# Running the first four weight tiles of a stage together, input chunk by input chunk, in a one-core transformer kernel

## The chip, the cores and the metric

The kernel runs on one core of a Trainium2 chip. The metric is the time of one execution on the device in microseconds (us). The core's engines are called PE (TensorE, matmuls), DVE (VectorE), ACT (ScalarE), POOL (GpSimd) and SP (SyncE, which issues most DMAs); ACTq and SPq are the queues that issue DMAs.

## The reference, cut to what matters

`x` is 512 tokens by 1024 features. Two blocks run one after the other, then a hybrid mixer, a cross attention over a memory of 256 tokens, and a gated feed-forward. Every matrix product that the change touches takes the output of an RMS norm:

```python
y = x * rsqrt(mean(x * x, axis=-1) + eps) * g       # the norm
h = modulate(y, shift, scale)                       # in the first two blocks
# block 0: nsa_mixer(h): h @ w_in (1024 x 2608), rotary, three attentions, @ w_out
# block 1: swa_sink_mixer(h): q, k, v = h @ w_in (1024 x 1280), rotary, window attention, @ w_out
a = relu(h @ w_up); y = (a * a) @ w_down            # MLP of both blocks, 4096 hidden
proj = h @ w_in_2; q = h @ wq; kv = mem_n @ wkv     # hybrid mixer, cross attention
h @ ffn_w_up_2                                      # feed-forward, 2 x 2816
```

## The kernel before, in words

Activations are held transposed, as eight **chunks** of 128 features by 512 tokens. fp32 accuracy comes from splitting: a chunk is a rounded high part `ah` and a rest `al`, a weight a high part `wh` and a rest `wl`. A **unit** is a weight tile of 1024 x 128; its product takes, for each of the eight chunks, three matmuls (lines 702 to 704: wh by ah, wl by ah, wh by al), so 24 in one PSUM bank. There are some 309 units, and they pass through a ring of four slots (`RING = 4`): SP loads `raw` (L533), ACT rounds it to `wh` (L1806, in `highs`, which first waits until the unit four before has been used), POOL subtracts to get `wl` (L642), PE multiplies (`gemm`, L720, unit by unit, chunks inside), DVE evacuates the bank. PE waits in `bank_free` for the bank of four units before, and on `lo_done` for the weights.

`norm` on DVE (L1176) makes the chunks one at a time: L1184 scales, ACT rounds (L1843 or L1845), L1198 or L1196 makes the rest and signals `a_ready`. `gemm` with `ready=` waits for each chunk in turn, so the first unit after a norm goes at the pace of the norm.

What hangs on a unit's end differs by stage. In the two MLPs (`mlp`, L925 on PE, L1457 on DVE, L1976 on ACT) eight "up" units are followed at once by eight "down" units that read the hidden chunks. For each "up" unit DVE does relu (L1465), square (L1467), waits for ACT's rounding to `hh` (L1985), and subtracts to `hl` (L1469), which signals `hid_made`; in the first MLP it also adds one modulation step (L1488, L1491). ACT's order is written out: round the weights of unit c+4, then wait for DVE's square of unit c, then `hh` of c. In the sliding-window stage (`swa_in`) pairs of units are rotated by DVE (`rotary`, L1304 to L1318), ACT rounds them and issues their writes to DRAM (`rotated`, L1867 to L1879: 8 DMAs of 256 KB for k, 4 for each of the four q pairs), and SP waits for the k and first q writes before it loads them back (L536, L540) and before it issues the next weight tiles. In `nsa_in` ACT writes the first rotated pair and units 3 and 4 to scratch (L1896, L1900), and SP waits for both before it issues the loads that follow.

At a stage's end `highs_and_squares` (L1821) does for each of the last eight units: `highs` of unit c+4, then the square of the evacuated chunk c. `root` (L1829) takes the square root of their sum.

Of the kernel before, what the change touches and what calls it, by code (L numbers as in the profile page):

```python
# [73 lines left out]
def place_of_units():  # L74

    n = {name: FIRST[name] for name, _ in STAGES}
    of = list(range(UNITS))

    def stage(name, runs):
        got = [n[name] + a + k for a, count in runs for k in range(count)]  # L80
        of[n[name]:n[name] + len(got)] = got
    stage("nsa_in", ((0, 4), (12, 4), (16, 4), (20, 1), (4, 8)))
    stage("swa_in", ((8, 2), (10, 1), (0, 8)))
    for name in ("mlp0", "mlp1"):
        stage(name, [(8 * b, 8) for b in (0, 2, 1, 4, 3, 6, 5, 7)])
    stage("ffn", ((0, 16), (32, 8), (16, 16), (52, 8), (40, 12), (60, 8)))
    assert sorted(of) == list(range(UNITS))
    return of
# [151 lines left out]
def build(nc, src, out):  # L240
# [30 lines left out]
    cond = at("cond", k1 + 0.375, [P, DC])  # L271
    coef = at("coef", k1 + 0.4375, [P, 2, 6, DC])
    eps = at("eps", k1 + 0.875, [P, 1])
    neg_sinks = at("neg_sinks", k1 + 0.9375, [P, HEADS])
    ident_r = at("ident_r", k1 + 1, [P, P], F32R)
    mask_r = at("mask_r", k1 + 1.5, [P, 2, P], F32R)
# [412 lines left out]
    def _(pe):  # L689
# [30 lines left out]
        def gemm(first, count, high, low, turned=False, tokens=S, ks=DC, ready=None):  # L720
# [13 lines left out]
            over_units(pe, first, first + count, one)  # L734
            done[0] += count

        def gemm_pairs(first, pairs, high, low, tokens=S):

            for u in range(first, first + 2 * pairs, 2):
                n, slot = done[0], u % RING
                pe.wait_ge(lo_done, u + 2)
                for i in range(tokens // P):
                    if i % 2 == 0:
                        bank_free(n + i // 2)
                    o = ps[:, (n + i // 2) % RING, i % 2 * 256:i % 2 * 256 + 256].rearrange("p (a f) -> p a f", a=2)
                    t = slice(i * P, (i + 1) * P)
                    for k in range(DC):
                        nc.tensor.matmul(o, high[:, k, t], wh[:, slot:slot + 2, k], start=k == 0, stop=False)  # L750
                        nc.tensor.matmul(o, high[:, k, t], wl[:, slot:slot + 2, k], start=False, stop=False)
                        mm = nc.tensor.matmul(o, low[:, k, t], wh[:, slot:slot + 2, k], start=False, stop=k == DC - 1)
                mm.then_inc(unit_used, 2)
                done[0] += tokens // P // 2
# [170 lines left out]
        def mlp(name, hid0):  # L925
            u = FIRST[name]
            for b, (what, grp) in enumerate(MLP_BLOCKS):

                def sums():
                    if name == "mlp0" and b:  # L930
                        pe.wait_ge(adc_used, 8 * b)
                        ada(ps[:, 6, 8 * b:8 * b + 8], acc_mlp[:, (b - 1) % 2])
                if what == "up":
                    gemm(u, 4, ah, al, ready=(a_ready, A_READY[name]))
                    sums()
                    gemm(u + 4, 4, ah, al)
                elif b == 7:
                    gemm_squared(u, hh, hl, 0, ready=(hid_made, hid0 + 8 * grp), midway=sums)
                else:
                    gemm(u, 4, hh, hl, ready=(hid_made, hid0 + 8 * grp))  # L940
                    sums()
                    gemm(u + 4, 4, hh, hl)
                u += 8
# [10 lines left out]
            ada(ps[:, 7, 8 * k:8 * k + 8], acc_in)  # L954

        u = FIRST["nsa_in"]
        gemm(u, RING, ah, al, ready=(a_ready, 0))
        gemm(u + RING, 4, ah, al)
        gemm_pairs(u + 8, 2, ah, al)
        ada_in_sum(0)  # L960
# [28 lines left out]
        square_sums()  # L989
        mlp("mlp0", 0)  # L990
        square_sums()
        gemm(FIRST["swa_in"], 2, ah, al, ready=(a_ready, A_READY["swa_in"]))
        gemm(FIRST["swa_in"] + 2, 1, ah, al, turned=True)
        gemm(FIRST["swa_in"] + 3, 8, ah, al)
        attention(PLAN_SWA)
        gemm_squared(FIRST["swa_out"], ah, al, 0, ready=(o_split, 2 * GROUPS))
        square_sums()
# [1 line left out]
        square_sums()  # L999

        u = FIRST["mix_in"]
        gemm(u, 7, ah, al, ready=(a_ready, A_READY["mix_in"]))

        pe.wait_ge(evac, done[0] - 6)
        for c in range(2):
# [64 lines left out]
        head_spread(3)  # L1070
        gemm_squared(FIRST["mix_out"], ah, al, 1, ready=(mix_ready, 0))

        gemm(FIRST["xq"], 8, ah, al, ready=(a_ready, A_READY["xq"]))
        square_sums(MEM)
        gemm(FIRST["kv"], 7, mh, ml, tokens=MEM, ready=(a_ready, A_READY["mem"]))
        gemm_pairs(FIRST["kv"] + 7, 4, mh, ml, tokens=MEM)
        gemm(FIRST["kv"] + 15, 1, mh, ml, tokens=MEM)
        pe.wait_ge(evac, done[0])
# [36 lines left out]
        for what, grp in FFN_BLOCKS:  # L1115
            n = FF_GROUPS[grp]
            if what == "up":
                gemm(u, 2 * n, ah, al, ready=(a_ready, A_READY["ffn"]))
                u += 2 * n
            else:  # L1120
                ready = (hid_made, 64 + sum(FF_GROUPS[:grp]))
# [8 lines left out]
    def _(dve):  # L1130
# [430 lines left out]
        ada_read_out(11, ps[:, 6, 56:64])  # L1561
        ada_coef(1, 5)
        rotary(pair_s)
        v.tensor_copy(vv[:, 0, :, 0:P], bank().rearrange("p (i f) -> p i f", i=SC)).then_inc(evac, 1)
        for _ in range(4):
            rotary(pair_s, query=True)
        attention(PLAN_SWA)
        copy_out()
# [218 lines left out]
    def _(act):  # L1787
# [33 lines left out]
        def highs_and_squares(u, out_t, bank0):  # L1821

            for c in range(DC):
                highs(u + RING + c, u + RING + c + 1)
                squares(out_t[:, c:c + 1], (evac, lambda _: bank0 + c + 1), count=1,
                        added=6 * summed[0] + max(c - 2, 1) if c >= 2 else None)
            summed[0] += 1
# [180 lines left out]
        u = FIRST["swa_in"]  # L2008
        highs(u + RING, u + RING + 2)
        rotated(6, pair_s)  # L2010
        highs(u + RING + 2, u + RING + 3)
        for p in range(4):
            highs(u + RING + 3 + 2 * p, u + RING + 5 + 2 * p)
            rotated(7 + p, pair_s, grp=p)
        n += UNITS_SWA_IN
        attention(PLAN_SWA)
# [221 lines left out]
```

## Time and profile before

| | us |
|---|---|
| median of three runs | 2417.26 (2416.27 to 2418.76) |
| the profiled execution, its own time | 2418.09 |
| its span in the trace | 2416.3 |
| PE busy | 2104.6 (87%) |
| DVE busy | 1137.4 (47%) |
| POOL busy | 901.5 (37%) |
| ACT busy | 693.4 (29%) |

The granted TensorE clock was 0.904 of full speed on the mean. A matmul's busy time overlaps the next one's, so a busy PE is not one at its peak, and the shares are a mean over stages with different limits.

### The profile page before, as it was taken

The page shows a single profiled execution, that of the slowest core. Times are in us where ns is not written, and L with a number is a line of the kernel's source. Part 1 is how long each engine was busy: PE and PEld are TensorE (multiplying, and loading weights), DVE is VectorE, ACT ScalarE, POOL GpSimd, SP SyncE. Part 2 cuts the span into 40 slices and gives each one's busy share as a digit, 9 for nine tenths or more (in the row PEclk, how much of TensorE's full clock was granted, in tenths as well). Part 3 has the DMA queues.
Part 4 walks back from the last instruction along what each step waited for, and adds up shares of the span by engine and source line. Part 5 has one row for each costly group of instructions (what it writes and reads, how often), then busy time and mean ns, then how long its engine had stood idle before and what let it go on. Part 6 is the DMA issues. An engine that isn't in the chain of part 4 may idle for free.

```text
span 2416.3 us, 27295 instructions
## 1 busy us (share of the span) xinstructions
PE 2104.6 (87%) x10492; PEld 1722.9 (71%) x10492; DVE 1137.4 (47%) x1672; ACT 693.4 (29%) x1195; POOL 901.5 (37%) x513
## 2 busy tenths in 40 slices
PE   2968679997999997958799999797689878999997
PEld 2766667775888885846588888676577646888886
DVE  6424545637564564444544244336432224626354
ACT  2112244533222223135322222323132313222222
POOL 1223244432544542256244444333034403444442
PEclk9968569997999997979899999899699879999998
DMA  6543521222655540432133333222022302333331
GB/s 245 193 156 104 189 86 47 71 71 87 200 184 177 195 141 27 149 134 83 53 96 96 96 96 96 78 70 79 1 96 89 113 9 79 96 96 96 96 96 61
DMA packets 79770, 255.33 MB, mean 106 GB/s; under 512 B 10536, under 2 KB 11048, under 8 KB 79272
## 3 DMA queue, kind: packets, MB, share of 16 engines
q1 hardware_dynamic: 70480, 237.86, 29.8%
q10 hardware_dynamic: 9176, 15.89, 1.9%
q8 instruction: 79, 1.29, 0.2%
q14 instruction: 35, 0.29, 0.0%
HBM read 235.21 MB, written 18.51 MB: 105 GB/s over the span
## 4 chain that ended last, share of the span: by engine, by line
PE 46%; issue 29%; POOL 11%; DVE 7%; DMA 3%; ACT 2%; ACTq 1%; SPq 0%; POOLq 0%; DVEq 0%
PE ps L702 11%; PE ps L704 11%; PE ps L703 11%; POOL wl L642 10%; PE ps L911 2%; DMA raw<-in_units 2%; PE ps L857 2%; PE ps L883 2%; DMA qscr<-rot_ls 1%; POOL pr L663 1%; PE ps L1108 1%; PE ps L842 1%; DVE tt L1184 1%; PE ps L1085 1%; ACTq L1875 1%
## 5 line engine op out<-in xcount | busy, mean ns | idle before, releaser
L642 POOL TENSOR_TENSOR wl<-raw,wh 128x1024 fp32r<-128x1024 f32 x309 | 764.2, 2477 | 1371.5 <-ACT wh L1806 1371.5
L1806 ACT CAST wh<-raw 128x1024 fp32r<-128x1024 f32 x309 | 323.4, 1051 | 1286.4 <-PE ps L704 1031.6
L702 PE MATMUL ps<-ah,wh 128*128 128x512 f32 x1496 | 596.5, 399 | 30.0 <-DVE al L1198 18.7
L703 PE MATMUL ps<-ah,wl 128*128 128x512 f32 x1496 | 588.4, 393 | 0.0
L704 PE MATMUL ps<-al,wh 128*128 128x512 f32 x1496 | 588.2, 393 | 0.0
L702 PEld LDWEIGHTS ps<-ah,wh 128*128 128x128 f32 x1496 | 284.2, 190 | 107.4 <-issue 21.1
L704 PEld LDWEIGHTS ps<-al,wh 128*128 128x128 f32 x1496 | 284.6, 190 | 60.3
L703 PEld LDWEIGHTS ps<-ah,wl 128*128 128x128 f32 x1496 | 285.2, 191 | 56.9 <-issue 0.7
L702 PE MATMUL ps<-hh,wh 128*128 128x512 f32 x688 | 269.2, 391 | 4.0 <-DVE hl L1763 4.0
L703 PE MATMUL ps<-hh,wl 128*128 128x512 f32 x688 | 268.2, 390 | 0.0
L704 PE MATMUL ps<-hl,wh 128*128 128x512 f32 x688 | 268.2, 390 | 0.0
L1469 DVE TENSOR_TENSOR hl<-rs,hh 128x512 fp32r<-128x512 f32 x64 | 135.6, 2119 | 43.9 <-ACT hh L1985 43.9
L702 PEld LDWEIGHTS ps<-hh,wh 128*128 128x128 f32 x688 | 129.5, 188 | 32.0 <-DVE hl L1763 5.2
L704 PEld LDWEIGHTS ps<-hl,wh 128*128 128x128 f32 x688 | 129.5, 188 | 27.2
L703 PEld LDWEIGHTS ps<-hh,wl 128*128 128x128 f32 x688 | 129.6, 188 | 26.7
L857 PE MATMUL ps<-ks,qs 128*128 128x256 f32 (+3 forms) x384 | 95.8, 356 | 28.0 <-ACT pr L1941 14.7
L1941 ACT ACTIVATE pr<-ps,st 128x512 f32<-128x512 f32 (+1 forms) x192 | 94.3, 504 | 68.5 <-DVE st L1375 47.2
L1375 DVE TENSOR_REDUCE st<-ps 128x1 f32<-128x512 f32 (+1 forms) x192 | 78.2, 449 | 51.3 <-PE ps L860 43.9
L661 POOL TENSOR_SCALAR pr<-pr,st,gates 128x512 f32<-128x512 f32 (+3 forms) x128 | 75.9, 608 | 57.5 <-DVE st L1402 56.9
L857 PEld LDWEIGHTS ps<-ks,qs 128*128 128x128 f32 x384 | 65.3, 210 | 38.4 <-issue 17.4
L1476 DVE TENSOR_TENSOR y<-ps,y 128x512 f32<-128x512 f32 x32 | 22.1, 692 | 123.1 <-PE ps L704 123.1
L762 PE MATMUL ps<-sq,sm 128*32 128x128 f32 x440 | 33.8, 393 | 52.7 <-ACT sq L1818 48.0
(270 smaller groups left out, 2617.4 us busy)
## 6 DMA issues: line engine op xcount, KB each, us to landing
raw<-in_units SPq DMA_DIRECT2D x309, 512.0 KB, 3.5
ada_mlp<-in_ada SPq DMA_DIRECT2D x56, 512.0 KB, 3.4
ada_in<-in_ada SPq DMA_DIRECT2D x24, 512.0 KB, 7.7
ada<-in_ada SPq DMA_DIRECT2D x16, 512.0 KB, 5.3
qs<-qscr SPq DMA_DIRECT2D x32, 256.0 KB, 2.7
ks<-kscr SPq DMA_DIRECT2D x12, 512.0 KB, 3.9
x<-in_xT SPq DMA_DIRECT2D x1, 2048.0 KB, 13.3
kscr<-rot_h ACTq DMA_DIRECT2D x8, 256.0 KB
```

The costliest lines, as they stand in the source:

```text
L642: nc.gpsimd.tensor_tensor(wl[:, slot], raw[:, slot], wh[:, slot].bitcast(F32), ALU.subtract).then_inc(lo_done, 1)
L661: op = nc.gpsimd.tensor_scalar(o, o, st[:, 2, n % 4, i:i + 1], gates[:, i, c:c + 1], ALU.mult, ALU.mult)
L702: nc.tensor.matmul(out_ap, wh[:, slot, k], high[:, k0 + k], start=first and k == 0, stop=False)
L703: nc.tensor.matmul(out_ap, wl[:, slot, k], high[:, k0 + k], start=False, stop=False)
L704: mm = nc.tensor.matmul(out_ap, wh[:, slot, k], low[:, k0 + k], start=False, stop=last and k == ks - 1)
L857: nc.tensor.matmul(o, qs[:, j, i * P:(i + 1) * P], ks[:, slot, part, k0 * P:k1 * P], start=part == 0, stop=False)
L883: mm = nc.tensor.transpose(ps[:, plan.t_bank + b, col + c * P:col + (c + 1) * P], pr[:, n % 3, at0:at0 + P], small("ident"))
L911: mm = nc.tensor.matmul(ps[HD * h:HD * h + HD, bank, q[0] * P:(q[-1] + 1) * P], vv[:, kind, kb, col_v:col_v + HD], pt[:, n[h] % 4, place[k ...
L1375: op = v.tensor_reduce(st[:, 0, s, i:i + 1], ps[:, plan.s_bank(w, b), col:col + (k1 - k0) * P], X, ALU.max, negate=True)
L1469: v.tensor_tensor(hl[:, c], t, hh[:, c].bitcast(F32), ALU.subtract).then_inc(hid_made, 1)
L1806: a.copy(wh[:, slot], raw[:, slot]).then_inc(hi_done, 1)
L1941: a.activation(pr[:, n % 3, b * S + col:b * S + col + width], ps[:, plan.s_bank(w, b), col:col + width], ACT.Exp, bias=shift[:, i:i + 1], ...
```

## The change

A new function `gemm_wide` multiplies several units with the chunks as the outer loop. It is used for the first four units after each of the eight norms (for the kv product with 256 tokens). In `swa_in` the order of units becomes k, k, q, q, v, q x6 instead of k, k, v, q x8, with PE's, DVE's and ACT's order changed to fit. One ACT instruction, a square root of `eps` into a new [128, 1] tile `warm`, is put between `highs` and `squares` of the last unit in `highs_and_squares`.

```diff
-    stage("swa_in", ((8, 2), (10, 1), (0, 8)))
+    stage("swa_in", ((8, 2), (0, 2), (10, 1), (2, 6)))
...
+        def gemm_wide(first, count, high, low, ready, tokens=S):
+
+            n0 = done[0]
+            pe.wait_ge(lo_done, first + count)
+            for i in range(count):
+                bank_free(n0 + i)
+            for k in range(DC):
+                pe.wait_ge(ready[0], ready[1] + k + 1)
+                for i in range(count):
+                    o, slot = ps[:, (n0 + i) % RING, 0:tokens], (first + i) % RING
+                    nc.tensor.matmul(o, wh[:, slot, k], high[:, k], start=k == 0, stop=False)
+                    nc.tensor.matmul(o, wl[:, slot, k], high[:, k], start=False, stop=False)
+                    mm = nc.tensor.matmul(o, wh[:, slot, k], low[:, k], start=False, stop=k == DC - 1)
+                    if k == DC - 1:
+                        mm.then_inc(unit_used, 1)
+            done[0] += count
...
-                    gemm(u, 4, ah, al, ready=(a_ready, A_READY[name]))
+                    if b == 0:
+                        gemm_wide(u, 4, ah, al, (a_ready, A_READY[name]))
+                    else:
+                        gemm(u, 4, ah, al)
...
-        gemm(FIRST["swa_in"], 2, ah, al, ready=(a_ready, A_READY["swa_in"]))
-        gemm(FIRST["swa_in"] + 2, 1, ah, al, turned=True)
-        gemm(FIRST["swa_in"] + 3, 8, ah, al)
+        gemm_wide(FIRST["swa_in"], 4, ah, al, (a_ready, A_READY["swa_in"]))
+        gemm(FIRST["swa_in"] + 4, 1, ah, al, turned=True)
+        gemm(FIRST["swa_in"] + 5, 6, ah, al)
...
         rotary(pair_s)
+        rotary(pair_s, query=True)
         v.tensor_copy(vv[:, 0, :, 0:P], bank().rearrange("p (i f) -> p i f", i=SC)).then_inc(evac, 1)
-        for _ in range(4):
+        for _ in range(3):
...
                 highs(u + RING + c, u + RING + c + 1)
+                if c == DC - 1:
+                    a.activation(warm[:], eps[:], ACT.Sqrt)
                 squares(out_t[:, c:c + 1], (evac, lambda _: bank0 + c + 1), count=1,
...
         highs(u + RING, u + RING + 2)
         rotated(6, pair_s)
-        highs(u + RING + 2, u + RING + 3)
         for p in range(4):
-            highs(u + RING + 3 + 2 * p, u + RING + 5 + 2 * p)
+            highs(u + (6, 8, 11, 13)[p], u + (8, 11, 13, 15)[p])
             rotated(7 + p, pair_s, grp=p)
```

The same replacement of the first `gemm` by `gemm_wide` stands at `nsa_in`, `mix_in`, `xq`, `kv` and `ffn`.

## Rows read from the trace of the kernel before

**Rows 1.** The page's busy time by engine, and its group of matmuls on L704.

```profile
PE 2104.6 (87%) x10492; PEld 1722.9 (71%) x10492; DVE 1137.4 (47%) x1672; ACT 693.4 (29%) x1195; POOL 901.5 (37%) x513
...
L704 PE MATMUL ps<-al,wh 128*128 128x512 f32 x1496 | 588.2, 393 | 0.0
```

**Rows 2.** Windows: us, busy time (count) by engine, granted PE clock, DMA share, GB/s.

```profile
572.43:598.10 25.67, 25.32 (x97) 19.19 (x97) 21.66 (x24) 8.63 (x11) 7.47 (x3) 0.88 0.24 82
583.59:597.19 13.60, 13.60 (x61) 11.26 (x60) 11.10 (x10) 3.79 (x5) 7.03 (x3) 1.00 0.45 154
1196.73:1222.39 25.66, 24.26 (x97) 18.41 (x98) 18.78 (x21) 8.63 (x11) 7.46 (x3) 0.94 0.17 44
1852.61:1867.33 14.72, 14.72 (x97) 14.10 (x98) 5.91 (x15) 5.17 (x8) 6.31 (x3) 0.80 0.17 48
```

**Rows 3.** Timeline of PE at the start of the first MLP (start, duration).

```profile
573.00 0.63 PE L703 MATMUL ps<-ah,wl 128*128 128x512 f32 x1
573.42 0.63 PE L704 MATMUL ps<-al,wh 128*128 128x512 f32 x1
```

**Rows 4.** Timeline of DVE, ACT, POOL after the first MLP's first unit (start, duration).

```profile
581.97 0.69 DVE L1465 TENSOR_SCALAR rs<-ps 128x512 f32<-128x512 f32 x1 [1.12 <-PE ps L704]
582.02 1.05 ACT L1806 CAST wh<-raw 128x1024 fp32r<-128x1024 f32 x1 [2.41 <-PE ps L704]
582.69 0.69 DVE L1467 TENSOR_TENSOR rs<-rs 128x512 f32<-128x512 f32 x1
583.15 2.49 POOL L642 TENSOR_TENSOR wl<-raw,wh 128x1024 fp32r<-128x1024 f32 x1 [31.67 <-ACT wh L1806]
583.42 0.62 ACT L1985 CAST hh<-rs 128x512 fp32r<-128x512 f32 x1 [0.34 <-DVE rs L1467]
584.07 2.12 DVE L1469 TENSOR_TENSOR hl<-rs,hh 128x512 fp32r<-128x512 f32 x1 [0.69 <-ACT hh L1985]
```

**Rows 5.** Timeline of DVE within the first MLP, and of POOL and DVE in nsa_in.

```profile
861.92 1.27 DVE L1491 SCALAR_TENSOR_TENSOR acc_mlp<-ada_mlp,cond,acc_mlp 128x1024 f32<-128x1024 f32 x1
863.21 0.69 DVE L1465 TENSOR_SCALAR rs<-ps 128x512 f32<-128x512 f32 x1
...
233.96 4.63 POOL L642 TENSOR_TENSOR wl<-raw,wh 128x1024 fp32r<-128x1024 f32 x1 [13.44 <-ACT wh L1806]
...
233.70 2.71 DVE L1347 SCALAR_TENSOR_TENSOR xb_l<-x,sm,xb_h 128x124 fp32r<-128x124 f32 x8
```

**Rows 6.** Timeline of DVE and ACT in nsa_in, after its second unit.

```profile
72.40 0.69 DVE L1304 TENSOR_TENSOR pair<-ps,trig 128x512 f32<-128x512 f32 x1 [6.66 <-PE ps L704]
...
77.08 1.66 ACTq L1896 DMA_DIRECT2D cscr<-pair  x2
...
83.26 1.28 ACTq L1900 DMA_DIRECT2D cscr<-vtmp  x2
```

**Rows 7.** Timeline in swa_in: k rotation, k writes, q reads, first score matmul.

```profile
976.47 0.69 DVE L1304 TENSOR_TENSOR pair_s<-ps,trig 128x512 f32<-128x512 f32 x1 [4.70 <-PE ps L704]
...
986.51 8.39 ACTq L1879 DMA_DIRECT2D kscr<-rot_ls  x4
...
1022.58 1.81 SPq L536 DMA_DIRECT2D qs<-qscr  x4
...
1043.85 0.58 PE L857 MATMUL ps<-ks,qs 128*128 128x256 f32 x1 [13.28 <-DVE pair_s L1307]
```

**Rows 8.** ACT at the end of nsa_out and of the second MLP, and all loads of L1833.

```profile
548.01 1.04 ACT L1806 CAST wh<-raw 128x1024 fp32r<-128x1024 f32 x1 [3.86 <-PE ps L704]
548.96 0.62 ACT L1818 ACTIVATE sq<-y 128x512 f32<-128x512 f32 x1
549.61 1.28 ACT L1833 ACT_TABLE_LOAD   x1
550.90 0.37 ACT L1833 ACTIVATE rs<-ps,eps 128x128 f32<-128x128 f32 x1
...
1551.16 0.37 ACT L1833 ACTIVATE rs<-ps,eps 128x128 f32<-128x128 f32 x1 [0.55 <-PE ps L762]
...
L1833 ACT ACT_TABLE_LOAD  x5: 1283/1283/1283, 24.2 to 2403.1; - x5
```

More of the change, by code:

```diff
@@ L273, in build @@
     eps = at("eps", k1 + 0.875, [P, 1])
+    warm = at("warm", k1 + 0.90625, [P, 1])
     neg_sinks = at("neg_sinks", k1 + 0.9375, [P, HEADS])
@@ L956, in _ @@
         u = FIRST["nsa_in"]
-        gemm(u, RING, ah, al, ready=(a_ready, 0))
+        gemm_wide(u, RING, ah, al, (a_ready, 0))
         gemm(u + RING, 4, ah, al)
@@ L1001, in _ @@
         u = FIRST["mix_in"]
-        gemm(u, 7, ah, al, ready=(a_ready, A_READY["mix_in"]))
+        gemm_wide(u, 4, ah, al, (a_ready, A_READY["mix_in"]))
+        gemm(u + 4, 3, ah, al)
         pe.wait_ge(evac, done[0] - 6)
@@ L1071, in _ @@
         gemm_squared(FIRST["mix_out"], ah, al, 1, ready=(mix_ready, 0))
-        gemm(FIRST["xq"], 8, ah, al, ready=(a_ready, A_READY["xq"]))
+        gemm_wide(FIRST["xq"], 4, ah, al, (a_ready, A_READY["xq"]))
+        gemm(FIRST["xq"] + 4, 4, ah, al)
         square_sums(MEM)
-        gemm(FIRST["kv"], 7, mh, ml, tokens=MEM, ready=(a_ready, A_READY["mem"]))
+        gemm_wide(FIRST["kv"], 4, mh, ml, (a_ready, A_READY["mem"]), tokens=MEM)
+        gemm(FIRST["kv"] + 4, 3, mh, ml, tokens=MEM)
         gemm_pairs(FIRST["kv"] + 7, 4, mh, ml, tokens=MEM)
@@ L1117, in _ @@
             if what == "up":
-                gemm(u, 2 * n, ah, al, ready=(a_ready, A_READY["ffn"]))
+                if grp == 0:
+                    gemm_wide(u, 4, ah, al, (a_ready, A_READY["ffn"]))
+                    gemm(u + 4, 2 * n - 4, ah, al)
+                else:
+                    gemm(u, 2 * n, ah, al)
                 u += 2 * n
```

## The prediction

> **What bounds the kernel.** I read the page's busy times first: PE is busy 87% of the span [rows 1], so in most stages a microsecond of PE is a microsecond of the kernel. Then the windows around the norms. The first MLP's first four units take from 572.43 to 598.10, 25.67 us [rows 2], though in steady running 60 matmul intervals take 13.6 us, 0.227 each [rows 2], which makes 0.68 for a chunk's three, 5.44 for a unit and 21.8 for four. So 3.9 us are lost, and the change aims at that. The clock column says what the loss is made of: 0.88 of full, so PE ran at 1.2 GHz for about the first 6.0 us (0.12 x 2 x 25.67), having waited through the norm, and at 2.4 GHz after. At 1.2 GHz matmuls start 0.42 to 0.43 apart [rows 3], 1.28 for a chunk's three. Last, what hangs on a unit's end: the timelines of DVE, ACT and POOL [rows 4 to 7].
>
> **The change, part by part.**
>
> 1. Four units together. PE no longer starves for chunks, but the slow clock remains. With r us of it, four units take r + (32 - r/1.28) x 0.68. First MLP, r = 6.0: 24.6, gain 1.1. Second MLP, clock 0.94 over 25.66 us [rows 2], r near 2.9: 23.1, gain 2.5. The hybrid mixer, the cross attention's q and the feed-forward lie between; I take 1.9.
>
> 2. The fifth unit. Before, unit 1 ended three units early, and its slot was refilled in their shadow. Refilling takes a cast at 582.02 and a subtract that ends at 585.64, 3.6 us [rows 4], plus some 0.1 to release PE. Now after unit 1's last matmul only nine others follow, 2.0 us, of which about 0.5 pass until the cast starts (a matmul lasts 0.39 [rows 1]). Wait: 3.6 + 0.1 + 0.5 - 2.3 (nine and one interval) = 1.9 us, at each of the wide groups. So parts 1 and 2 cancel in the mixer, q and feed-forward: 0. For kv (256 tokens, intervals about half) four units take 14.72 now [rows 2] and gain at most 0.4, while nine matmuls cover only half as much, wait 3.0: **+2.7**.
>
> 3. The MLPs: DVE is late next. Call t = 0 the start of unit 1's relu. Before, units ended 5.44 apart, now 0.68 apart, so DVE, ACT and POOL start four units' work at once. The ninth unit ("down") starts at 3.75 + 4 x 5.44 = 25.5 and wants hidden chunk 8 at 30.3. Per unit: hh ends at h; the next weight cast, and POOL at h + 1.15 for 2.45; DVE does hl (0.69 when POOL is idle) and relu, and comes to the square at about h + 1.45, when POOL runs. A DVE instruction with two SBUF inputs waits until POOL ends and finishes 0.55 later (hl 584.07 for 2.12, POOL until 585.64 [rows 4]), so the square ends at h + 4.15 and the next hh at h + 4.8. Unit 2's hh ends at 7.9 (its square waits for the second subtract, 4.2 to 6.7), unit 8's at 7.9 + 6 x 4.8 = 36.7, hl at 37.4: PE waits 7.2. Second MLP: 7.2 + 1.9 - 2.5 = **+6.6**. In the first MLP DVE has the modulation step too, 1.27, and no slack already: it ends at 863.19 and the next relu starts at 863.21 [rows 5]. It also holds POOL back, as the run of DVE instructions from 233.70 that made a subtract take 4.63 [rows 5]; period 5.5 to 5.6, I take 5.5: hh(2) at 8.5, hl(8) at 42.2, wait 11.9. First MLP: 11.9 + 1.9 - 1.1 = **+12.7**.
>
> 4. The clock after those waits. PE is nearly idle for 7 and 12 us and should fall to 1.2 GHz. After the norms the low clock lasted 2.9 to 6.0 us of PE's work, costing half of it. Two times, with the slow last chunks: **+5** (0 if the waits do not lower it).
>
> 5. swa_in. The k pair was ready at 976.47 [rows 7], about 15.0 after the stage's first matmul (9.5 for unit 1 by the first MLP's pace, 581.97 - 572.43, and 5.44 for unit 2). Now it is ready 1.1 before the four end, at 24.6 - 1.1 = 23.5. The 8 k writes queue behind it (ACT's last four issues take 8.39, so the queue is full), the q writes behind them, SP reads q back only at 1022.58, behind SP stand the next weights, behind these the third q's rotation, and the scores start at 1043.85 [rows 7]. That q comes earlier in the order helps nothing, its writes queue behind k's. The whole chain moves: +8.4; I take **+8.2**.
>
> 6. nsa_in. The second unit is ready 7.6 later than 72.40 by the same sum with r = 7. The rotation takes 4.6 until the issue at 77.08, which takes 1.66; then ACT casts two more weights before issuing vtmp's writes, so these come near 87.5 instead of 83.26 [rows 6]. All of SP's later loads stand behind them: **+4** (0 to 6).
>
> 7. The table load. Of L1833's five loads [rows 8] the first is outside; three lie at nsa_out, swa_out and xo, one at the end. `highs` of the last round waits for the last unit (cast at 548.01 <-PE), and the new instruction is behind it, so the load is not within the last unit but after it. Now cast start to square start is 0.95, square to root 1.94 [rows 8]; without a load square to root is about 1.17 (0.62 and the 0.55 of idle at 1551.16). After: cast 1.05, load 1.28, warm about 0.2, then 1.17: 3.7 against 2.9, +0.8 three times. Where no load was needed the warm costs 0.2 three times. At the very end no weights are left to cast, so the load is really hidden, -0.8. **+2.3** (-3 to +4).
>
> The Trainium skill, page "ScalarE: Activation LUTs", section "What ACT_TABLE_LOAD costs", puts a drain of about 1.38 us behind each load, 2.66 in all. The trace disagrees: the root at 550.90 starts as the 1.28 end. By the page the three moved loads would cost 1.4 more each and the sum would be 46.
>
> Sum: 2.7 + 6.6 + 12.7 + 5 + 8.2 + 4 + 2.3 = 41.5. Against the profiled execution's own time, 2418.1, that is 2459.6; the median of the runs lies 0.8 below that execution, so 2459.
>
> **The rivals.**
>
> A. Everything that hangs on a unit's end stays hidden, and PE's own time alone counts. Place: from unit 1's end to unit 5's start and to the ninth unit. It decides if refill takes under 2.3 us and hidden chunk 8 is there by 30.3. Then seven gains of 1.0 to 2.5 and 0.4, some 12, and with the loads hidden another 3: **2403**, faster. Against: refill takes 3.6 in a row [rows 4]. For: POOL, DVE and ACT are far from busy [rows 1].
>
> B. DVE wins the port. POOL's subtract starts only 0.3 before the square in my count. If the square comes first, a unit takes DVE 2.75 (3.9 in the first MLP) and nothing is late for "down": 41.5 - 7.2 - 11.9 - 5 = 17.4, **2435**. The Trainium skill, page "SBUF — State Buffer", section "Who interferes with whom", says whoever issues first holds the shared ports for its whole instruction, so 0.3 us of order decides; both directions are seen in rows 4 and 5.
>
> C. The queues absorb nsa_in and swa_in (DMAs shorter when they stand apart): 41.5 - 12 = 29.5, **2447**.
>
> D. The low clock stays through the waits and long after, and DVE and POOL alternate worse: **2470**.
>
> E. The compiler puts the load ahead of the wait, so the change does what it says there: -5.5, 2453, inside the range.
>
> **How the numbers follow.** The forecast with E has 0.55, B 0.14, C 0.10, D 0.10, A 0.08, no change 0.03. Bounds of the forecast: clock 0 (-5), first MLP at period 4.8 (-4), nsa_in 0 (-4), swa_in 5 (-3), gains at their best (-3) give 2440; B takes the lower end to 2434; D with 2 more the upper to 2472. A change under 0.2% (4.8 us) can't be told from none; slower by more 0.88, same 0.03, faster 0.09.
>
> **What would show it.** The four units in about 24.6 and 23.1 us, and a POOL subtract alone before the fifth unit. In both MLPs the ninth unit's L702 waiting for hl, 7 and 12 us, and the clock at 0.5 there. The k rotation about 8 later after its stage's first matmul, scores too. L1833's loads gone to the warm line, three of them behind a cast that waited for PE. I am wrong if PE runs into "down" without a gap, or if the fifth unit follows within 0.3.

## The result, and the profile after

The changed kernel takes **2474.11 us** (median of six runs, 2469.95 to 2477.16) against 2416.56 of the kernel before (six runs, 2412.99 to 2418.76): 1.0238 times the time, 95% interval 1.0225 to 1.0251. It is 57.5 us slower; the forecast was 2459, 41.5 slower, and its range ended at 2472. The profiled execution took 2475.20 with a span of 2473.4. Lines of the kernel after stand 1 to 31 higher than before: the unit's matmuls are L703 to L705, those of four units together L748 to L750, POOL's subtract L643, the weight cast L1835, relu, square and hl of the MLPs L1493, L1495 and L1497.

The page's busy times, to hold against [rows 1]:

```profile
PE 2116.0 (86%) x10492; PEld 1738.5 (70%) x10492; DVE 1160.3 (47%) x1672; ACT 692.2 (28%) x1202; POOL 909.1 (37%) x513
```

DVE has the same 1672 instructions and 23 us more busy time, POOL 8 us more: they block each other oftener. The mean granted clock fell from 0.904 to 0.897. Where the time went is read from marks that both traces have: the root of each norm (L1833 before, L1864 after), the first score matmul of each attention (L857 before, L875 after), the end. The shift of after against before grows, from mark to mark, by:

| stretch | forecast | measured |
|---|---|---|
| nsa_in and what follows it, to the first scores | +4 | +12.96 |
| that attention and nsa_out | +0.8 | -0.85 |
| the norm between | 0 | -0.33 |
| both MLPs | +24.7 (waits less gains 19.3, clock 5, load 0.4) | +21.79 (first 14.55, second 7.24) |
| swa_in, to its scores | +8.2 | +8.50 |
| its attention and swa_out | +0.8 | +2.74 |
| mixer, and q of the cross attention | +0.2 | -0.04 |
| k, v, cross attention, xo | +3.5 | +3.99 |
| feed-forward and the end | -0.8 | +8.12 |

With +0.21 at the first root they make the 57.1 by which the spans differ. Two lines of nine are wrong, nsa_in and the feed-forward.

**The four units.** Windows of the first MLP's and the second's wide group with the wait for the fifth unit behind it, and of kv's; columns as in [rows 2]:

```profile
584.42:610.33 25.91, 24.12 (x97) 19.47 (x97) 11.33 (x15) 6.25 (x8) 2.60 (x2) 0.91 0.00 1
1234.50:1259.71 25.21, 23.43 (x97) 19.00 (x97) 11.32 (x15) 6.25 (x8) 2.60 (x2) 0.94 0.00 1
1897.57:1914.36 16.79, 14.15 (x97) 13.98 (x97) 6.15 (x16) 5.66 (x9) 2.50 (x2) 0.84 0.00 1
```

These windows hold the group and the refill. Then PE's timeline around the fifth unit of the first MLP, and ahead of its ninth:

```profile
608.15 0.39 PE L750 MATMUL ps<-al,wh 128*128 128x512 f32 x1
...
610.33 0.47 PE L703 MATMUL ps<-ah,wh 128*128 128x512 f32 x1 [1.79 <-POOL wl L643]
...
637.82 0.50 PE L703 MATMUL ps<-hh,wh 128*128 128x512 f32 x1 [2.04 <-DVE hl L1497]
...
643.14 0.79 PE L703 MATMUL ps<-hh,wh 128*128 128x512 f32 x1 [4.35 <-DVE hl L1497]
...
648.47 0.80 PE L703 MATMUL ps<-hh,wh 128*128 128x512 f32 x1 [3.68 <-DVE hl L1497]
```

The last matmul of the group starts at 608.15 and the next at 610.33, 2.18 apart where 0.23 is normal: 1.95 us of refill (forecast 1.9). The group took 608.38 - 584.42 = 24.0 us (forecast 24.6), 1.7 less than in [rows 2], and the second MLP's 23.3 (forecast 23.1). Then the ninth unit waits for hidden chunks at three matmuls.

**Why they are late.** DVE and POOL in the first MLP, then in the second (timeline; start, duration):

```profile
616.17 1.28 DVE L1519 SCALAR_TENSOR_TENSOR acc_mlp<-ada_mlp,cond,acc_mlp 128x1024 f32<-128x1024 f32 x1
616.56 3.15 POOL L643 TENSOR_TENSOR wl<-raw,wh 128x1024 fp32r<-128x1024 f32 x1 [3.56 <-ACT wh L1835]
...
618.08 2.17 DVE L1495 TENSOR_TENSOR rs<-rs 128x512 f32<-128x512 f32 x1
...
623.46 2.17 DVE L1495 TENSOR_TENSOR rs<-rs 128x512 f32<-128x512 f32 x1
...
1264.61 2.39 POOL L643 TENSOR_TENSOR wl<-raw,wh 128x1024 fp32r<-128x1024 f32 x1 [2.24 <-ACT wh L1835]
1264.94 2.62 DVE L1495 TENSOR_TENSOR rs<-rs 128x512 f32<-128x512 f32 x1
...
1269.58 2.61 DVE L1495 TENSOR_TENSOR rs<-rs 128x512 f32<-128x512 f32 x1
```

A unit comes every 5.38 us (623.46 - 618.08) in the first MLP and every 4.64 (1269.58 - 1264.94) in the second, against the 5.5 and 4.8 of the forecast. The square starts 0.33 after the subtract (forecast 0.3), waits through it and ends 0.56 behind it. PE takes 5.44 for a unit, so DVE, which got four units at once, wins back next to nothing a unit in the first MLP and 0.8 in the second, and is still behind at the ninth unit in both. What PE waited for in all, from the view of waits (us in total, times, longest):

```profile
PE ps L703 <- DVE hl L1497: 15.4, 5, 4.4
...
PE ps L703 <- POOL wl L643: 13.4, 8, 2.6
...
PE ps L703 <- DVE hl L1792: 10.6, 4, 5.5
```

The first row is both MLPs, the second the refills, the third the feed-forward, which had 4.0 before. The clock follows (windows):

```profile
640.11:653.76 13.65, 6.94 (x16) 5.01 (x17) 9.45 (x9) 3.23 (x4) 6.55 (x3) 0.50 0.67 234
1288.64:1295.47 6.83, 3.38 (x8) 2.74 (x9) 3.40 (x3) 1.67 (x2) 2.04 (x2) 0.50 0.21 77
```

PE ran at 1.2 GHz there and at 2.4 on both sides. It worked for 6.9 and 3.4 us of the two stretches, half of which is lost: 3.5 + 1.7 = 5.2 (forecast 5).

**nsa_in.** DVE, ACT, POOL and SP from the k pair to the first modulation step; [rows 6] answer:

```profile
81.22 0.69 DVE L1332 TENSOR_TENSOR pair<-ps,trig 128x512 f32<-128x512 f32 x1 [15.70 <-PE ps L750]
...
84.47 2.89 DVE L1338 TENSOR_TENSOR pair<-pair 128x512 f32<-128x512 f32 x1
...
87.39 1.66 ACTq L1927 DMA_DIRECT2D cscr<-pair  x2
...
90.13 0.80 ACTq L1931 DMA_DIRECT2D cscr<-vtmp  x1
...
97.54 2.65 SPq L587 DMA_DIRECT2D x<-cscr  x4
...
112.01 2.73 DVE L1363 TENSOR_SCALAR acc_in<-ada_in,cond 128x1024 f32<-128x1024 f32 x1 [23.45 <-DMA ada_in<-in_ada]
```

and the kernel before at the two last points:

```profile
87.11 2.65 SPq L586 DMA_DIRECT2D x<-cscr  x4
...
101.51 2.81 DVE L1335 TENSOR_SCALAR acc_in<-ada_in,cond 128x1024 f32<-128x1024 f32 x1 [17.63 <-DMA ada_in<-in_ada]
```

The stage's first matmul, in the kernel before and in the one after, with the four subtracts that the latter waits for:

```profile
56.01 0.77 PE L702 MATMUL ps<-ah,wh 128*128 128x512 f32 x1 [6.37 <-DVE al L1198]
...
48.14 9.72 POOL L643 TENSOR_TENSOR wl<-raw,wh 128x1024 fp32r<-128x1024 f32 x4 [47.72 <-ACT wh L1835]
...
57.92 0.79 PE L748 MATMUL ps<-ah,wh 128*128 128x512 f32 x1 [8.48 <-POOL wl L643]
```

Here alone `gemm_wide`'s wait for the weights of all four units ends last: the fourth subtract ends at 57.86, and the stage starts 1.9 later than before. The pair is 8.8 later (1.9 of it by that start, 6.9 by the four units), its last operation is now blocked by a subtract (2.89), so the pair's writes are 10.3 later, SP's release 10.4, the modulation step 10.5. The scores are 13.2 later; the stretch from the modulation step to them takes 217.2 us before and 219.8 after, but also 219.5 in experiment 9, which leaves nsa_in as it was, so these last 2.7 us are not told from spread. The v writes are issued 6.0 later only: 83.26 in [rows 6] against 89.25.

**swa_in.** The k pair starts to rotate at 1010.51, 22.7 after the stage's first matmul at 987.85 (forecast 23.5; 15.1 before), the scores at 1078.88, 8.5 later against that matmul than before.

**The feed-forward.** DVE and POOL near the end of the first up block, and the clock at the down block (timeline, then a window):

```profile
2163.40 2.10 DVE L1789 TENSOR_TENSOR uc<-uc 128x512 f32<-128x512 f32 x1
2165.65 2.39 DVE L1791 CAST hh<-uc 128x512 f32 x1
...
2174.03 2.09 DVE L1789 TENSOR_TENSOR uc<-uc 128x512 f32<-128x512 f32 x1
...
2162.55 5.21 POOL L643 TENSOR_TENSOR wl<-raw,wh 128x1024 fp32r<-128x1024 f32 x2 [5.30 <-ACT wh L1835]
...
2179.52:2189.76 10.24, 4.76 (x10) 3.31 (x11) 6.88 (x10) 1.68 (x2) 0.26 (x1) 0.50 0.14 50
```

Two subtracts run in a row over the multiply and the cast. A pair of units takes DVE 10.63 us (2174.03 - 2163.40), PE 2 x 5.44 = 10.88. That was not in the forecast at all.

**The table load.** ACT at nsa_out's end, against [rows 8]:

```profile
559.60 1.05 ACT L1835 CAST wh<-raw 128x1024 fp32r<-128x1024 f32 x1 [3.85 <-PE ps L705]
560.66 1.28 ACT L1855 ACT_TABLE_LOAD   x1
561.95 0.20 ACT L1855 ACTIVATE warm<-eps 128x1 f32<-128x1 f32 x1
562.06 0.61 ACT L1847 ACTIVATE sq<-y 128x512 f32<-128x512 f32 x1
563.22 0.37 ACT L1864 ACTIVATE rs<-ps,eps 128x128 f32<-128x128 f32 x1 [0.55 <-PE ps L780]
```

Cast to root is 3.62 against 2.89, so +0.73 (forecast 0.8): the load stands behind the cast, and the cast behind the last unit. At the very end, square to root went from 1.94 to 1.33.

### The profile page after: what moved, and what is told of

Its sections match the earlier page's. It is cut to its first block, busy times and chain, and to the rows that moved or that the text cites. A ratio compares the mean times of both kernels' runs of the same rounds, so it can differ in the third digit from the quotient of the medians.

```text
span 2473.4 us, 27241 instructions
## 1 busy us (share of the span) xinstructions
PE 2116.0 (86%) x10492; PEld 1738.5 (70%) x10492; DVE 1160.3 (47%) x1672; ACT 692.2 (28%) x1202; POOL 909.1 (37%) x513
## 3 DMA queue, kind: packets, MB, share of 16 engines
q8 instruction: 81, 1.33, 0.2%
## 4 chain that ended last, share of the span: by engine, by line
PE 41%; issue 31%; POOL 10%; DVE 10%; DMA 3%; ACT 2%; ACTq 1%; SPq 0%; DVEq 0%; POOLq 0%
POOL wl L643 9%; PE ps L703 9%; PE ps L705 9%; PE ps L704 9%; PE ps L929 2%; DMA raw<-in_units 2%; PE ps L875 2%; PE ps L901 2%; DMA qscr<-rot_ls 1%; PE ps L1132 1%; PE ps L748 1%; POOL pr L664 1%; PE ps L749 1%; PE ps L750 1%; ACTq L1906 1%
## 5 line engine op out<-in xcount | busy, mean ns | idle before, releaser
L643 POOL TENSOR_TENSOR wl<-raw,wh 128x1024 fp32r<-128x1024 f32 x309 | 771.1, 2503 | 1423.0 <-ACT wh L1835 1422.9
L1835 ACT CAST wh<-raw 128x1024 fp32r<-128x1024 f32 x309 | 322.2, 1052 | 1245.3 <-PE ps L705 864.6
L703 PE MATMUL ps<-ah,wh 128*128 128x512 f32 x1272 | 500.0, 393 | 10.7 <-POOL wl L643 10.7
L705 PE MATMUL ps<-al,wh 128*128 128x512 f32 x1272 | 496.7, 391 | 0.0
L704 PE MATMUL ps<-ah,wl 128*128 128x512 f32 x1272 | 496.7, 390 | 0.0
L703 PE MATMUL ps<-hh,wh 128*128 128x512 f32 x688 | 272.3, 396 | 25.9 <-DVE hl L1497 15.4
L703 PEld LDWEIGHTS ps<-ah,wh 128*128 128x128 f32 x1272 | 240.3, 189 | 64.8 <-issue 7.1
L704 PEld LDWEIGHTS ps<-ah,wl 128*128 128x128 f32 x1272 | 240.3, 189 | 50.3 <-issue 0.7
L705 PEld LDWEIGHTS ps<-al,wh 128*128 128x128 f32 x1272 | 239.8, 189 | 50.2
L704 PE MATMUL ps<-hh,wl 128*128 128x512 f32 x688 | 270.2, 393 | 0.0
L705 PE MATMUL ps<-hl,wh 128*128 128x512 f32 x688 | 270.1, 393 | 0.0
L703 PEld LDWEIGHTS ps<-hh,wh 128*128 128x128 f32 x688 | 130.8, 190 | 57.0 <-DVE hl L1497 17.8
L705 PEld LDWEIGHTS ps<-hl,wh 128*128 128x128 f32 x688 | 130.7, 190 | 27.7
L704 PEld LDWEIGHTS ps<-hh,wl 128*128 128x128 f32 x688 | 131.0, 190 | 27.0
L1497 DVE TENSOR_TENSOR hl<-rs,hh 128x512 fp32r<-128x512 f32 x64 | 115.5, 1805 | 44.1 <-ACT hh L2016 44.1
L875 PE MATMUL ps<-ks,qs 128*128 128x256 f32 (+3 forms) x384 | 96.2, 357 | 26.5 <-ACT pr L1972 14.4
L748 PE MATMUL ps<-ah,wh 128*128 128x512 f32 x224 | 93.9, 419 | 25.8 <-DVE al L1226 8.7
L750 PE MATMUL ps<-al,wh 128*128 128x512 f32 x224 | 92.1, 411 | 0.0
```

Of the source, the lines that this page charges most:

```text
L643: nc.gpsimd.tensor_tensor(wl[:, slot], raw[:, slot], wh[:, slot].bitcast(F32), ALU.subtract).then_inc(lo_done, 1)
L703: nc.tensor.matmul(out_ap, wh[:, slot, k], high[:, k0 + k], start=first and k == 0, stop=False)
L704: nc.tensor.matmul(out_ap, wl[:, slot, k], high[:, k0 + k], start=False, stop=False)
L705: mm = nc.tensor.matmul(out_ap, wh[:, slot, k], low[:, k0 + k], start=False, stop=last and k == ks - 1)
L748: nc.tensor.matmul(o, wh[:, slot, k], high[:, k], start=k == 0, stop=False)
L750: mm = nc.tensor.matmul(o, wh[:, slot, k], low[:, k], start=False, stop=k == DC - 1)
```

## The experiments

Each kernel is the one after with the edit shown, unless another base is named; `...` stands for lines left out. Stretches are read from the same marks. Where no number of runs is given, the time is that of one execution; six of the kernel after spread over 7 us.

**1. Both MLPs unit by unit.**

```diff
-                    if b == 0:
-                        gemm_wide(u, 4, ah, al, (a_ready, A_READY[name]))
-                    else:
-                        gemm(u, 4, ah, al)
+                    gemm(u, 4, ah, al, ready=(a_ready, A_READY[name]))
```

> The kernel after, with the first four units of both MLPs one by one again. Theory (what hangs on a unit's end comes late: the fifth unit's refill, then DVE's hidden chunks, then the slow clock): the first MLP gives back 14.5 us and the second 7.2, everything else stays, so about 2452 against 2474; no gap of PE ahead of the ninth unit, no slow clock there. Rival (the four units together are themselves slower on PE, through their waits and their change of weights): PE's time for the first four units gets shorter and the ninth unit's wait stays, so the MLPs give back only the part that lies before the fifth unit, under 3 us each, 2468 or more.

2450.67. Against the kernel before, the first MLP stands at +0.08 and the second at +0.11, so they gave back 14.5 and 7.1. No row with hl as releaser is left in either block, and the clock is whole from 584.9 to 950.1. The rival is out.

**2. nsa_in and the feed-forward unit by unit.** The same edit at two other places.

> The kernel after, with the first four units of nsa_in and of the feed-forward one by one again. Theory: the compressed-branch scores start 13.0 us earlier (10.5 of it is there at the first modulation step, because the k pair's writes to DRAM are done before the v writes are issued), and the feed-forward is 8.1 to 8.9 shorter, its gaps ahead of the down units (2.35 and 6.11 us) gone and the low clock behind them too: 2452 or so. Rival (the order of the units costs PE the time itself, or the 13 us at nsa's scores come from elsewhere, such as the later weights of the branch): nsa gives back no more than the 1 or 2 us by which its four units differ, the feed-forward's gaps stay, 2468 or more.

2449.77. nsa's scores stand 0.25 ahead of the kernel before (13.2 given back), the feed-forward 2.1 ahead (10.2 given back). That it stands ahead has two reasons, which the kernel after shares: the final load is hidden (0.6), and a short stretch at 1.2 GHz, 3.41 us at 2370 in the kernel before, is missing (1.7). So the change's own cost in the feed-forward is 8.1 + 0.6 + 1.7 = 10.4. SP is released at 86.50, its pair written from 76.45.

**3. swa_in as before.** Order of units and single units restored.

> The kernel after, with swa_in's units one by one and in the old order (k pair, v, q). Theory: the scores of the sliding window start 8.5 us earlier against the stage's first matmul, and the attention loses another 1 or 2 of its 2.7, so about 2464. Rival (the 8.5 come from the fifth unit's refill and its slow clock, or from the earlier stages' lag carried in): under 3 us come back, 2471 or more.

2464.21. The scores come exactly as before (-0.01 in the stretch, so 8.5 given back) and the attention keeps 0.84 of its 2.74. That second part proves nothing about swa_in: experiments 1 and 7 leave it as in the kernel after and show 0.97 and 0.82 there.

**4. Without the table-loading activation.**

```diff
-                if c == DC - 1:
-                    a.activation(warm[:], eps[:], ACT.Sqrt)
```

> The kernel after, without the instruction that loads the table (an activation that no output depends on; nothing else is left out). Theory: nsa_out, swa_out and xo get 0.7 to 0.8 us shorter each, mlp0's, mlp1's and mix_out's ends 0 to 0.2, the very end of the program 0.8 longer, so 1.5 to 2.0 us in all, 2472 to 2473. Rival (the load is hidden as the change says and its cost lies elsewhere): all four get longer by 0.8, 2477.

2474.57, within the spread of the kernel after, so the total decides nothing. The rows do: square to root at nsa_out's end is 1.94 again (558.27 to 560.21). Cast to root is 2.89 at all three places, where the kernel after has 3.62, 3.63 and 3.86, and the final square to root 1.94. So the instruction costs 0.73 + 0.74 + 0.97 + 3 x 0.09 - 0.61 = 2.1 us, near what its theory says; other stretches moved by as much in this run (nsa's by -2.0, the feed-forward's by +2.1).

**5. swa_in's new order, the k pair alone together.**

```diff
-        gemm_wide(FIRST["swa_in"], 4, ah, al, (a_ready, A_READY["swa_in"]))
+        gemm_wide(FIRST["swa_in"], 2, ah, al, (a_ready, A_READY["swa_in"]))
+        gemm(FIRST["swa_in"] + 2, 2, ah, al)
```

> The kernel after, with swa_in's new order of units (k pair, first q pair, v, other q) kept, but only the k pair's two units run together and the q pair after it one by one. Theory (the chain through the DRAM writes starts at the k pair, which the four units together delay): the k pair is ready no later than before the change and the scores come 7.5 to 9.5 us earlier than in the kernel after, as with the whole stage undone; about 2465. Rival (the new order of units delays the scores, by q's writes queuing in another place): they come less than 3 us earlier, 2471 or more.

2462.44. From its timeline:

```profile
985.43 0.76 PE L748 MATMUL ps<-ah,wh 128*128 128x512 f32 x1 [2.91 <-DVE al L1227]
...
998.60 0.69 DVE L1333 TENSOR_TENSOR pair_s<-ps,trig 128x512 f32<-128x512 f32 x1 [2.58 <-PE ps L750]
...
1065.50 0.80 PE L875 MATMUL ps<-ks,qs 128*128 128x256 f32 x2 [12.28 <-DVE pair_s L1336]
```

The pair is there 13.2 after the first matmul, where it took 15.1 unit by unit and 22.7 with four together; the scores are 2.5 earlier than in the kernel before and 11.0 earlier than in the one after. So the new order doesn't delay the scores; they follow the k pair. Whether it helps them a little is open: with the first two units together the scores gain 1.2 and 0.7 in the old order (experiments 10 and 12) and 2.5 and 2.1 in the new one (here and experiment 11), and the stretch itself spread by 1.3 over seven kernels with the same swa_in.

**6. Without the square.** Left out is the square of the MLPs' hidden units (`tiny` is a spare column beside `eps`).

```diff
...
-                    v.tensor_scalar(t, bank(), 0.0, None, ALU.max).then_inc(evac, 1)
+                    b_ = bank()
+                    v.tensor_scalar(t, b_, 0.0, None, ALU.max).then_inc(hid_sq, 1)
+                    v.tensor_scalar(tiny[:], b_[:, 0:1], 0.0, None, ALU.max).then_inc(evac, 1)
                     dve.wait_ge(evac, banks[0])
-                    v.tensor_tensor(t, t, t, ALU.mult).then_inc(hid_sq, 1)
```

> The kernel after, leaving out the square of the MLPs' hidden units (the relu stands alone; in the square's place DVE runs a one-column operation that reads PSUM alone, so that it doesn't wait for POOL). Theory (DVE falls behind because its square waits for POOL's subtract, unit by unit): the wait ahead of the ninth unit is gone or under 1.5 us in both MLPs, with it the slow clock; the first MLP stands 0 to 3 us above the kernel before (the fifth unit's refill is left), the second -1 to +1.5; about 2454. Rival (refill, slow clock and the change of weights cost the time): both MLPs keep more than half of their 14.5 and 7.2, 2463 or more.

2461.49. The second MLP stands at -0.42: the wait, the slow clock and all of the 7.24 are gone, though refill is waited for as ever (1.9). The first keeps 8.85 where 0 to 3 was expected. Its DVE rows tell why:

```profile
618.31 1.46 DVE L1499 TENSOR_TENSOR hl<-rs,hh 128x512 fp32r<-128x512 f32 x1 [0.69 <-ACT hh L2018]
619.70 3.42 DVE L1521 SCALAR_TENSOR_TENSOR acc_mlp<-ada_mlp,cond,acc_mlp 128x1024 f32<-128x1024 f32 x1
...
627.72 1.45 DVE L1499 TENSOR_TENSOR hl<-rs,hh 128x512 fp32r<-128x512 f32 x1 [0.69 <-ACT hh L2018]
629.09 3.41 DVE L1521 SCALAR_TENSOR_TENSOR acc_mlp<-ada_mlp,cond,acc_mlp 128x1024 f32<-128x1024 f32 x1
```

Without the square the modulation step meets the subtract, every second time, and takes 3.4 in place of 1.3: 9.4 us for two units, 4.7 each. The lag starts at four units and is worked off only by 0.7 a unit, so 2.0 and 4.4 us of wait are left. Being held up is not tied to the square: here the multiply-add, which also has two SBUF inputs, takes it.

**7. v's writes on the other queue.**

```diff
+        for n in range(2):
+            sp.wait_ge(evac, 2 + n + 1)
+            sp.dma_start(cscr[1, 2 * n:2 * n + 2], vtmp[:, n]).then_inc(vc_kept, 16)
         sp.wait_ge(kc_kept, 32)
...
         highs(6, 8)
-        for n in range(2):
-            act.wait_ge(evac, 2 + n + 1)
-            act.dma_start(cscr[1, 2 * n:2 * n + 2], vtmp[:, n]).then_inc(vc_kept, 16)
```

> The kernel after, with the two DRAM writes of the compressed branch's v issued by SP in place of ACT (SP waits there for them anyhow). Theory (one queue's writes stand in a row, four of 256 KB at about 2.6 us each from 87.4): the v writes run beside the k pair's, SP is released 2 to 5 us earlier than at 97.54, and the first modulation step and nsa's scores come as much earlier, about 2470. Rival (the DMA engines are shared and the total of 1 MB sets the time): released no more than 1 us earlier, 2474. Third (the writes are late because DVE evacuates v late, not for the queue): also under 1 us, with the v writes issued after 89.

2479.53. SP's and ACT's queues:

```profile
86.63 1.85 SPq L585 DMA_DIRECT2D cscr<-vtmp  x2
97.87 2.65 SPq L590 DMA_DIRECT2D x<-cscr  x4
...
86.04 1.65 ACTq L1930 DMA_DIRECT2D cscr<-pair  x2
```

From the pair's first write to SP's release 11.8 us pass, more than the 10.2 with one queue. My theory of a queue in which the v writes stand last is out. The other kernels show what holds instead: the release comes 10.0 after the pair's first write in the kernel before (77.08 to 87.11), 10.2 in the one after, 10.1 in experiment 2, though v's writes are issued 6.2, 1.9 and 6.2 after the pair's. The release follows the pair's first write: in all 13 other kernels, which write over one queue, it comes 10.0 to 10.2 after it. Why it does is open. The rival, that the total of 1 MB sets the time, got its number right (97.87 against 97.54), and no run leaves v's writes out to tell it from the pair's being slow by themselves. In the kernel before the queue moves 102 GB/s while the pair's writes stand alone (80.5 to 83.2) and 251 once v's are there (84.2 to 86.6); in the one after it moves 97 at the end (94.6 to 96.6). Nor is it shown why this run is 5 us above the kernel after: its nsa_in is 1.7 shorter (the pair's rotation starts 1.3 earlier), and the rest is scattered over later stages.

**8. Two taps.** Left out is the third tap of the feed-forward's convolution.

```diff
-            link(v.scalar_tensor_tensor(out=o[:, 1:S], in0=bk[:, 0:S - 1], scalar=cw[:, 1, c], in1=o[:, 1:S],
-                                        op0=ALU.mult, op1=ALU.add))
-            v.scalar_tensor_tensor(out=o[:, 2:S], in0=bk[:, 0:S - 2], scalar=cw[:, 0, c], in1=o[:, 2:S],
+            v.scalar_tensor_tensor(out=o[:, 1:S], in0=bk[:, 0:S - 1], scalar=cw[:, 1, c], in1=o[:, 1:S],
                                    op0=ALU.mult, op1=ALU.add).then_inc(evac, 1)
...
-                    chain.enter(it, 12)
+                    chain.enter(it, 8)
```

> The kernel after, leaving out the third tap of the feed-forward's convolution: one DVE operation of 0.75 us and its wait less for every unit, about 1.6 to 1.8 us less for a pair of units. Theory (in the feed-forward DVE and POOL work off four units' lag at 10.6 us a pair against PE's 10.9, so the lag is still there at the down units): at 9.0 a pair the lag shrinks by 1.9 a pair, so the wait ahead of the second down unit goes from 6.1 to under 2 and the stage gets 5 to 7 us shorter, 2467 to 2469. Rival (the fifth unit's wait and the slow clock after the norm make the 8.1): the stage gets less than 1.5 us shorter.

2463.61. The feed-forward stands at +0.80 in place of +8.13. The wait at the fifth unit is still there (start to start 2.09); the 6.1 us ahead of the second down unit is gone, and the first waits no longer than before the change. So it was DVE's lag.

**9. The table load alone, ahead of the last cast.** On the kernel before.

```diff
             for c in range(DC):
+                if c == DC - 1:
+                    a.activation(warm[:], eps[:], ACT.Sqrt)
                 highs(u + RING + c, u + RING + c + 1)
```

> The kernel before, with the table-loading activation alone, one place earlier than in the change: ahead of the last round's weight cast, so ahead of the wait for the last unit. Theory (the load is in the way only where it stands behind that wait): nsa_out, swa_out and xo get 0.7 to 0.8 us shorter each and the end of the program 0.6 to 0.8, the other norms 0; together -2.5 to -3.2 us, a ratio of 0.9987 to 0.9990. Rival (a table load costs the same wherever it stands, or the cast behind it gets late): 0 or slower.

```profile
546.38 1.28 ACT L1826 ACT_TABLE_LOAD   x1
547.67 0.20 ACT L1826 ACTIVATE warm<-eps 128x1 f32<-128x1 f32 x1
550.22 1.04 ACT L1807 CAST wh<-raw 128x1024 fp32r<-128x1024 f32 x1 [2.34 <-PE ps L705]
551.17 0.63 ACT L1819 ACTIVATE sq<-y 128x512 f32<-128x512 f32 x1
552.35 0.37 ACT L1836 ACTIVATE rs<-ps,eps 128x128 f32<-128x128 f32 x1 [0.55 <-PE ps L763]
```

The load lies wholly in the wait for the last unit, and cast to root is 2.13 in place of 2.89. Its four stretches got shorter by 0.73, 0.87, 1.07 and 0.53, 3.2 together. In runs: 2415.63 (12 of them) against 2416.71, a ratio of 0.9992, interval 0.9982 to 1.0001. The rows show the saving, the total can't tell it from none.

**10. Two units together.** On the kernel before: two in place of four in nsa_in, swa_in (old order), second MLP, mixer, q, kv and feed-forward, first MLP unit by unit, load as in experiment 9; for instance:

```diff
-        gemm(u, RING, ah, al, ready=(a_ready, 0))
+        gemm_wide(u, 2, ah, al, (a_ready, 0))
+        gemm(u + 2, 2, ah, al)
```

> Two units together in place of four, in nsa_in, swa_in (old order of its units), second MLP, hybrid mixer, q, k and v of the cross attention and feed-forward; the first MLP unit by unit; the table load ahead of the last cast. Theory (the loss is in what hangs on a unit's end; with two together unit 1 ends some 4 us late and unit 2 a little early, so the k pairs come 1 to 2.5 us earlier and nothing falls behind): each of the seven groups gains 0 to 1.5 us, the loads 3, so 2402 to 2410 against 2416.5, 0.994 to 0.9975. Rival (any group run together starts the lag, and the third unit's refill is waited for as the fifth's was): 2416 or slower.

**2400.14** against 2416.71, 0.9926 (0.9913 to 0.9940): faster than both kernels, and by more than expected. Some 3 us of the 16.6 are the load's, by the rows of experiment 9. Against before: nsa_in +0.35, nsa_out's stretch -2.27, swa_in -1.21, swa_out's stretch -1.10, the norm behind it -0.91, second MLP -2.37, mixer -0.88, q -1.27, kv to xo -2.84, feed-forward -4.25. Its window over the second MLP's first units:

```profile
1191.43:1214.71 23.28, 23.28 (x97) 19.17 (x97) 18.15 (x20) 7.82 (x10) 7.68 (x3) 0.94 0.16 46
```

The 25.66 of [rows 2] became 23.28, as short as with four together, and PE is busy all through: no refill is waited for. Of the feed-forward's 4.25 some 1.7 is again the missing slow stretch at 2370; what makes it come and go was not tested. The -2.27 of nsa_out's stretch is within that stretch's spread (see the last section).

**11. The same in swa_in's new order.**

> The same as the run with two units together, but swa_in in the change's order (k pair, first q pair, v, other q). Theory (the k pair's end sets the scores, the order of the rest does nothing): within 0.7 us of that run. Rival (the 2.5 us by which the scores came earlier than in the kernel before, when only the k pair ran together, are the new order's): 1.5 to 2.5 us faster than that run.

2401.39 (2398.21 to 2405.31), 0.9936 (0.9923 to 0.9949) against before: not told apart from experiment 10, and not the 1.5 to 2.5 faster of the rival.

**12. Two together in the first MLP too.** Experiment 10 with that one group more.

> The run with two units together (old order of swa_in), with the first MLP's first two units together too. Theory (the first MLP's DVE has no slack to work off a lag, the second's has): unit 1's end comes some 4 us late, the ninth unit waits for its hidden chunk and the first MLP, -0.02 us against before when run unit by unit, gets 0 to 3 us longer or at best the same; the second keeps its gain of some 2. Rival (unit 1's lateness of 4 us is within what the stage bears, since unit 2 is early): the first MLP gains 1 to 2.5 us as the second did, about 2398.

2407.98. The first MLP gets 5.87 longer, the second keeps its -2.30. Timeline and window of PE:

```profile
625.85 0.80 PE L703 MATMUL ps<-hh,wh 128*128 128x512 f32 x1 [3.97 <-DVE hl L1499]
...
624.38:631.21 6.83, 5.36 (x13) 4.20 (x14) 3.28 (x5) 1.66 (x2) 2.41 (x1) 0.50 0.65 242
```

Theory right, size too small: I had not put in the slow clock behind the 4 us wait (half of 5.36, 2.7).

## Why the prediction was wrong

The sign and most of the mechanism were right, and the size was short by 16 us. Point by point, by its own steps:

1. **Four units together, and the fifth's refill** (steps 1 and 2). Right: 24.0 and 23.3 us against 24.6 and 23.1, refill 1.95 against 1.9, and mixer and q cancel to -0.04. kv with the table load +3.99 against 3.5.
2. **The MLPs** (step 3). Right, a little too dear. Waits at the ninth unit of about 10.6 (matmul starts 2.43, 4.75 and 4.31 apart, less their normal 0.23 and, at the slow clock, 0.43) against 11.9, and of 5.6 (starts 2.07 and 4.01 apart) against 7.2, which by the prediction's own 37.4 and 30.3 should read 7.1. Shown by experiments 1 and 6; experiment 6 adds that in the first MLP the modulation step is as much to blame as the square.
3. **The clock** (step 4). Right: 5.2 against 5.
4. **swa_in** (step 5). Right: 8.50 against 8.2, shown by experiments 3 and 5. The 2 us more in the attention behind it are not shown to come with the late k: they shrink to 0.8 in experiments 3 and 5, but also in 1 and 7 (0.97, 0.82), where k is as late as ever.
5. **nsa_in** (step 6). **The first step that failed**, +4 (0 to 6) where +12.96 came. I took the v writes, which come last, as what SP waits for, and let ACT's two casts between the two sets of writes absorb the pair's lateness. But SP is released 10.0 to 10.2 us after the pair's first write however close v's stand behind, in every kernel with one queue (what makes it so stays open). So the pair's 10.3 us went through undiminished. Two parts of them I had put at nothing: the wait for four weights before the first matmul (1.9), and a subtract in the pair's last operation (1.5); the four units themselves cost 6.9 against 7.6. The rest, 2.5, is not told from spread: six other kernels with this nsa_in stood at 8.8 to 12.2.
6. **The feed-forward** (steps 1 and 2: "parts 1 and 2 cancel"). **The second**, 0 where +8.13 came, 10.4 without the load's gain and the missing slow stretch. I worked out DVE's lag for the MLPs and not for this stage, which has 16 units to work it off. They don't suffice: at 10.6 us a pair against 10.9, eight pairs win back some 2 us. Refill 1.9, more wait at the down units by 1.1 and 5.9 (matmul starts 2.35 and 6.11 apart, the first 1.24 before), slow clock 2.4 (half of 4.76), less 0.7 for the four units (24.7 against 25.4 us): 10.6. Experiments 2 and 8 show it.
7. **The table load** (step 7). Right, 2.1 against 2.3 (three times 0.8 and 0.2 less 0.8 make 2.2). The Trainium skill, page "ScalarE: Activation LUTs", section "What ACT_TABLE_LOAD costs", has a drain of about 1.38 us behind the load; no such drain shows here: the next activation starts 0.01 us after the load's end (561.95), as in [rows 8].

Against the table's forecasts the two misses are 9.0 and 8.9 us, together 17.9, while the MLPs were 2.9 too dear. Of the rivals, B (DVE's square ahead of the subtract) was refused by order: the square starts 0.33 us after the subtract in the second MLP and 1.5 after it in the first; C (the queues absorb the lateness) by experiments 2 and 3; D came nearest in time, but not by its mechanism, the clock was as forecast.

Undoing the MLPs, nsa_in with the feed-forward, and swa_in, one at a time, gives back 23.4, 24.3 and 9.9 us, 57.7 together: the whole of the loss, if the spread of single runs is allowed for.

## What to carry to other kernels

Running several units with the chunks outside makes PE's stall at the first chunks vanish, and makes their ends fall together: ask of each engine behind how many units it must then catch up and how much faster than PE it is, for every stage and not only for those with a written due time. Two units together took the whole gain here (23.28 us as with four) with none of the refill wait; where DVE has no slack at all, even two cost 5.9. Where a group of DRAM writes is waited for as a whole, ask from which write its time counts: here it was the first, and that producer's lateness passed through. And a loop that takes several tiles at once waits for the last of their weights before its first matmul, which in one stage out of eight was a cost of its own.

## What the runs showed that was not expected

- The 1 MB of k and v in four writes is waited for until 10.0 to 10.2 us after the first is issued on one queue, whether the second two are issued 2 or 6 us behind, and until 11.8 after it over two queues.
- A subtract on POOL holds up more than DVE's operations with two SBUF inputs: the cast L1791, which has one, takes 2.39 us beside it in place of 0.43 before the change (at 2116.71). A relu that reads PSUM runs beside it unhindered (0.69 us at 622.74).
- PE's waits at the ninth and the down units (2 to 6 us each) went with 1.2 GHz over 6.8 to 13.7 us in both MLPs and the feed-forward; the refill waits of 1.9 us there left it at 2.4.
- Profiles of the same stage spread: to nsa's first scores by 4.2 us (+8.8 to +13.0 in seven kernels), in the stretch to nsa_out's root by 4.8 (-3.9 to +1.0 in the same seven), by 0.9 in several norms. A saving of one per mille could be read from rows and not from totals.
